# Two chunks per matmul in the triangular inverse of a chunked delta rule

## What is computed

```python
decay = jnp.exp(jnp.where(incl, gc[..., :, None] - gc[..., None, :], -jnp.inf))
kk = jnp.einsum('bhnid,bhnjd->bhnij', k, k)
a = jnp.where(strict, beta[..., :, None] * kk * decay, 0.0)
rhs = jnp.concatenate([beta[..., None] * v, (beta * jnp.exp(gc))[..., None] * k], axis=-1)
sol = lax.linalg.triangular_solve(eye + a, rhs, left_side=True, lower=True, unit_diagonal=True)
...
def step(state, xs):
    u_bar_c, w_c, qk_c, q_c, k_c, gl_c = xs
    u = u_bar_c - jnp.einsum('bhck,bhkv->bhcv', w_c, state)
    o = jnp.einsum('bhck,bhkv->bhcv', q_c, state) + jnp.einsum('bhcj,bhjv->bhcv', qk_c, u)
    state = gl_c[..., None, None] * state + jnp.einsum('bhck,bhcv->bhkv', k_c, u)
```

## Time and profile before

| | |
|---|---|
| median of three runs | 2509.23 us (2508.02 to 2509.98) |
| span of the profiled execution | 2508.8 us |
| PE busy | 2417.1 us, 96% of the span |
| DVE, ACT, POOL busy | 36%, 27%, 26% |
| one head of the delta loop | 94.4 us |
| one level of the inverse in it | 6.53 us |
| granted TensorE clock in the delta loop | full |

### The profile page before, as it was taken

One profiled execution on the slowest core, in us unless ns is written; L12 is line 12 of the kernel. 1 busy time (PEld: TensorE's weight loads), 2 busy tenths in 40 slices (PEclk: granted clock), 3 DMA queues, 4 the chain that ended last, 5 costly groups with the idle time before them and its releaser, 6 DMA issues.

```text
span 2508.8 us, 33006 instructions
## 1 busy us (share of the span) xinstructions
PE 2417.1 (96%) x12464; PEld 2031.8 (81%) x12464; DVE 905.7 (36%) x1069; ACT 688.6 (27%) x1204; POOL 660.2 (26%) x447
## 2 busy tenths in 40 slices
PE   5999999999799999999999999999899999999998
PEld 4787878787788888888888888887788888888887
DVE  4416262627554454454453112321422112211234
ACT  4333232324343543543452320011211001100112
POOL 6242232212111111111111323333233233323321
PEclk9999999999899999999999999999999999999999
DMA  5112121213010210220220443332111111111112
GB/s 119 37 42 85 51 84 50 75 42 109 18 59 17 59 59 12 63 59 10 66 67 26 160 137 119 119 101 70 39 49 43 50 50 42 50 51 45 48 44 82
DMA packets 219108, 157.30 MB, mean 63 GB/s; under 512 B 22744, under 2 KB 205208, under 8 KB 217520
## 3 DMA queue, kind: packets, MB, share of 16 engines
q1 hardware_dynamic: 206528, 106.05, 15.1%
q10 hardware_dynamic: 12528, 50.53, 5.6%
HBM read 137.49 MB, written 19.07 MB: 62 GB/s over the span
## 4 chain that ended last, share of the span: by engine, by line
PE 87%; DVE 5%; DVEq 2%; DMA 2%; issue 1%; ACT 1%; POOL 1%; SPq 0%; ACTq 0%; POOLq 0%
PE bank L198 62%; PE bank L988 5%; PE bank L1194 3%; PE bank L1204 3%; PE bank L1210 2%; DVEq L765 1%; DMA stat_b<-scr_stat 1%; PE bank L1151 1%; PE bank L602 1%; PE bank L1235 1%; DVE joint L769 1%; PE bank L1170 1%; PE bank L1222 1%; PE bank L1216 1%; PE bank L1176 1%
## 5 line engine op out<-in xcount | busy, mean ns | idle before, releaser
L198 PE MATMUL bank<-u_hi,w_hi 128*128 128x512 f32 x2176 | 907.3, 417 | 16.2 <-DVE u_lo L1642 7.2
L198 PE MATMUL bank<-u_hi,w_lo 128*128 128x512 f32 x2176 | 852.7, 392 | 0.0
L198 PE MATMUL bank<-u_lo,w_hi 128*128 128x512 f32 x2176 | 850.5, 391 | 0.0
L184 POOL CAST w_hi<-raw 128x1024 fp32r<-128x1024 f32 (+1 forms) x176 | 183.6, 1043 | 1768.6 <-PE bank L198 1522.7
L198 PEld LDWEIGHTS bank<-u_hi,w_hi 128*128 128x128 f32 x2176 | 411.7, 189 | 91.6 <-DVE u_lo L1642 8.8
L198 PEld LDWEIGHTS bank<-u_hi,w_lo 128*128 128x128 f32 x2176 | 409.5, 188 | 88.5
L198 PEld LDWEIGHTS bank<-u_lo,w_hi 128*128 128x128 f32 x2176 | 412.2, 189 | 69.4 <-issue 3.8
L186 POOL TENSOR_TENSOR w_lo<-raw,w_hi 128x1024 fp32r<-128x1024 f32 (+1 forms) x176 | 430.9, 2448 | 25.7 <-issue 0.7
L1756 DVE TENSOR_TENSOR tmp<-tmp,bank 128x512 f32<-128x512 f32 x44 | 30.2, 687 | 367.0 <-PE bank L198 367.0
L198 PE MATMUL bank<-v_hi,w_hi 128*128 128x512 f32 x352 | 137.3, 390 | 2.6 <-DVE tmp L1756 2.6
L198 PE MATMUL bank<-v_hi,w_lo 128*128 128x512 f32 x352 | 137.0, 389 | 0.0
(11 more groups left out here) (238 smaller groups left out, 2792.4 us busy)
## 6 DMA issues: line engine op xcount, KB each, us to landing
raw<-in_w_in SPq DMA_DIRECT2D x84, 512.0 KB, 3.8
stat_b<-scr_stat ACTq DMA_DIRECT2D x12, 1024.0 KB, 6.7
row<-scr_rows ACTq DMA_DIRECT2D x24, 512.0 KB, 4.9
raw<-in_w_gate SPq DMA_DIRECT2D x22, 512.0 KB, 3.8
raw<-in_w_up SPq DMA_DIRECT2D x22, 512.0 KB, 3.9
scr_gate<-tmp ACTq DMA_DIRECT2D x16, 512.0 KB, 2.9
tmp<-scr_gate ACTq DMA_DIRECT2D x16, 512.0 KB, 4.2
raw<-in_w_down SPq DMA_DIRECT2D x16, 512.0 KB, 3.7
```

The source lines that it names most:

```text
L184: nc.gpsimd.tensor_copy(hi[:, 0:kt, :], raw[slot][:, 0:kt, :])
L198: last = nc.tensor.matmul(bank[dst][:, :], wpart[slot][wp][:, k, :], rhs[ap][:, k, half * HALF:(half + 1) * HALF], start=k == 0 and (wp, a ...
```

## The change

Two neighbouring chunks share one matmul. Of `neg_a` only the right columns of the current level are taken, 64 of each chunk, and packed into `a_right` [128, 512]: a stationary tile of 128 columns then holds two chunks. The moving operand is the left columns of `inv` of both chunks (128 columns). The product has the wanted blocks of the two chunks on its diagonal; ACT copies only these into `half_pair`, a tile [128, 4, 128] whose other blocks are zeroed once. The transposes take only the right columns of `inv` (packed by DVE into `inv_right`), two chunks in one. The `d` matmul multiplies the paired transpose with `half_pair`, and the result lies in the bank as before, so that the masked copy is unchanged.

```diff
+        half_pair = dt_("half_pair", [P, NCH // 2, P])
+        a_right, inv_right = dt_("a_right", [P, HALF]), dt_("inv_right", [P, HALF])
...
         STEPS_AT = {4: ["ss"], 8: ["vt0"], 9: ["vt1"], 15: ["kt0"], 16: ["kt1", "kk0"], 17: ["kk1"], 18: ["qk0"],
-                    19: ["qk1"], 21: ["t00"], 22: ["t01"], 42: ["ub0", "ub1", "wt0", "wt1"], 61: ["os"], 63: ["on"]}
+                    19: ["qk1"], 20: ["t00"], 21: ["t01"], 41: ["tt0", "tt1"], 43: ["ub0", "ub1", "wt0", "wt1"],
+                    62: ["os"], 63: ["on"]}
         for level in range(1, 7):
-            for n_, x_ in enumerate("ydt"):
-                STEPS_AT[24 + 3 * (level - 1) + n_] = [f"{x_}{level}0", f"{x_}{level}1"]
+            STEPS_AT[22 + 3 * (level - 1)] = [f"y{level}"]
+            STEPS_AT[23 + 3 * (level - 1)] = [f"p{level}"]
+            STEPS_AT[24 + 3 * (level - 1)] = [f"d{level}0", f"d{level}1"]
         for c_ in range(NCH):
-            STEPS_AT[44 + 2 * c_] = [f"a{c_}"]
-            STEPS_AT[45 + 2 * c_] = [f"b{c_}"]
+            STEPS_AT[45 + 2 * c_] = [f"a{c_}"]
+            STEPS_AT[46 + 2 * c_] = [f"b{c_}"]
...
+            elif step[0] == "y":
...
+                pe.wait_ge(dl["ar"], h * 6 + level)
+                for q in range(NCH // 2):
+                    if level > 1 and q % 2 == 0:
+                        pe.wait_ge(dl["dtm"], n + (q // 2 - 1))
+                    last = mm(by_block(chunk(bank[Y0], q), level), chunk(a_right, q),
+                              side_columns(inv[:, 2 * q * P:2 * (q + 1) * P], level, 0), start=True, stop=True)
+            elif step[0] == "p":
+                level = int(step[1])
+                pe.wait_ge(dl["ir"], h * 6 + level)
+                for q in range(NCH // 2):
+                    last = tr(chunk(bank[X0], q), chunk(inv_right, q), ident[:, :])
+            elif step[0] == "d":
                 level, half = int(step[1]), int(step[2])
+                if half == 0:
+                    pe.wait_ge(dl["yc"], h * 6 + level)
+                    pe.wait_ge(dl["prc"], h * 6 + level)
+                for q in (2 * half, 2 * half + 1):
+                    last = mm(bank[Z0 + half][:, (q % 2) * P:(q % 2 + 1) * P], chunk(inv_t, q), half_pair[:, q, :],
+                              start=True, stop=True)
...
+            elif step[:2] == "tt":
+                half = int(step[2])
+                pe.wait_ge(dl["dtm"], h * 12 + (11 + half))
+                for c in range(4 * half, 4 * half + 4):
+                    last = tr(bank[X0 + half][:, (c % 4) * P:(c % 4 + 1) * P], chunk(inv, c), ident[:, :])
...
+            elif step[0] == "y":
+                level = int(step[1])
+                act.wait_ge(dl["y"], h * 6 + level)
+                y_now = bank[Y0][:, :].rearrange("p (q j) -> p q j", j=P)
+                f(half_pair[0:64, :, 0:64], y_now[0:64, :, 0:64], ACT.Copy)
+                f(half_pair[64:P, :, 64:P], y_now[64:P, :, 64:P], ACT.Copy).then_inc(dl["yc"], 1)
+                if level < 6:
+                    f(by_block(a_right[:, :], level + 1), side_columns(neg_a[:, :], level + 1, 1), ACT.Copy).then_inc(dl["ar"], 1)
+            elif step[0] == "p":
+                act.wait_ge(dl["pr"], h * 6 + int(step[1]))
+                f(inv_t[:, 0:HALF], bank[X0][:, :], ACT.Copy).then_inc(dl["prc"], 1)
...
+                if half == 1 and level < 6:
+                    dve.drain()
+                    v.tensor_copy(by_block(inv_right[:, :], level + 1),
+                                  side_columns(inv[:, :], level + 1, 1)).then_inc(dl["ir"], 1)
+            elif step == "t01":
+                dve.wait_ge(dl["t0c"], two + 2)
+                v.tensor_copy(by_block(inv_right[:, :], 1), side_columns(inv[:, :], 1, 1)).then_inc(dl["ir"], 1)
```

More of the change, by code:

```diff
@@ L1184, in delta_pe @@
                 last.then_inc(dl["t0"], 1)
-            elif step[0] in "ydt" and step[1] in "123456":
-                level, half = int(step[1]), int(step[2])
[L1187 to L1211, removed]
@@ new lines, in delta_pe @@
+            elif step[0] == "y":
+                level = int(step[1])
+                n = h * 12 + 2 * (level - 1)
+                if level == 1:
+                    pe.wait_ge(dl["t0c"], two + 2)
+                    pe.wait_ge(dl["a"], two + 2)
+                pe.wait_ge(dl["ar"], h * 6 + level)
[4 more added lines that the diff above has]
+                              side_columns(inv[:, 2 * q * P:2 * (q + 1) * P], level, 0), start=True, stop=True)
+                last.then_inc(dl["y"], 1)
+            elif step[0] == "p":
[3 more added lines that the diff above has]
+                    last = tr(chunk(bank[X0], q), chunk(inv_right, q), ident[:, :])
+                last.then_inc(dl["pr"], 1)
+            elif step[0] == "d":
+                level, half = int(step[1]), int(step[2])
+                if half == 0:
+                    pe.wait_ge(dl["yc"], h * 6 + level)
+                    pe.wait_ge(dl["prc"], h * 6 + level)
+                if level == 1:
+                    pe.wait_ge(dl["pt"], two + (half + 1))
+                for q in (2 * half, 2 * half + 1):
+                    last = mm(bank[Z0 + half][:, (q % 2) * P:(q % 2 + 1) * P], chunk(inv_t, q), half_pair[:, q, :],
+                              start=True, stop=True)
+                last.then_inc(dl["dt"], 1)
+            elif step[:2] == "tt":
[3 more added lines that the diff above has]
+                    last = tr(bank[X0 + half][:, (c % 4) * P:(c % 4 + 1) * P], chunk(inv, c), ident[:, :])
+                last.then_inc(dl["tt"], 1)
@@ L1212, in delta_pe @@
             elif step[:2] == "ub":
                 half = int(step[2])
-                pe.wait_ge(dl["ttc"], h * 12 + (11 + half))
+                pe.wait_ge(dl["ttc"], two + (half + 1))
                 for c in range(4 * half, 4 * half + 4):
@@ L1286, in delta_act @@
                 f(c4(inv, half), bank[X0 + half][:, :].rearrange("p (c t) -> p c t", t=P), ACT.Copy).then_inc(dl["t0c"], 1)
[L1287 to L1295, removed]
+                if half == 1:
+                    act.wait_ge(dl["a"], two + 2)
+                    f(by_block(a_right[:, :], 1), side_columns(neg_a[:, :], 1, 1), ACT.Copy).then_inc(dl["ar"], 1)
+            elif step[0] == "y":
+                level = int(step[1])
+                act.wait_ge(dl["y"], h * 6 + level)
[7 more added lines that the diff above has]
+                f(inv_t[:, 0:HALF], bank[X0][:, :], ACT.Copy).then_inc(dl["prc"], 1)
+            elif step[:2] == "tt":
+                half = int(step[2])
+                act.wait_ge(dl["tt"], two + (half + 1))
+                f(inv_t[:, half * HALF:(half + 1) * HALF], bank[X0 + half][:, :], ACT.Copy).then_inc(dl["ttc"], 1)
             elif step[:2] == "ub":
@@ L1443, in prepare_vec @@
                               ident[:, :].unsqueeze(1).broadcast_to([P, NCH, P]))
+                v.memset(half_pair[:, :, :], 0.0)
             dve.drain()
```

8 lines of the change are left out of this document (5 added, 3 removed).

## The result

The changed kernel takes **2452.24 us** (median, 2451.58 to 2453.41) against 2508.65 for the kernel before in the same runs: ratio 0.9772, 95% interval 0.9758 to 0.9786. It is 56 us faster; 73 were forecast, and the time lies inside the range of 2418 to 2462. It lies 2 us above the stretch that the forecast held most likely, 2425 to 2450.

A forecast was written before the change was run, and what follows sets the result against it. The inverse was taken as bound by PE issue: 8 x (12.26 saved - 3.04 new waits) = 73.8, less 0.5 for zeroing, is 73.3 us; span 2508.8 becomes 2435.5, median 2436 us, range 2418 to 2462.

The forecast's parts named there:

- What bounds the kernel: Delta loop's inverse: bound by what PE has to issue (busy 93.49 of 94.40 us per head), not its ACT/DVE chain.
- the price of the paired matmuls: y and d in each level: eight records cost 0.82 us instead of 1.70; four transposes cost 0.36 instead of 0.79.
- The rival by which the price follows the columns: y and d stay at 1.70 us with strided columns; each head 1.34 slower, 2520 us; chance 0.03.
- Net saving without waits: PE per head: 13.14 us saved in six levels, less 0.88 for the last full transpose: 12.26, or 98.1 in eight.
- The sum of the new waits: Four tighter hand-overs to PE: 1.35 + 0.79 + 0.60 + 0.30 = 3.04 us per head.
- first y: Head's first y waits for a_right, copied behind the last t0 copy: idle 0.68 us, with restart 0.79.
- first d: Level 1's d stands behind a dense copy on ACT as well: 0.60 us with the restart.
- second y: y's second half after the first d waits for merges; the first takes 0.73 instead of 0.44: 0.3 us with restart.
- item 1: d waits for ACT's copy of the packed transposes: 0.27 us in each of levels 2 to 6, 1.35 per head.
- the rival of slow packed copies: a_right's short runs cost ACT twice 0.63 us, delaying d, some 25 us in all: 2461, range 2450 to 2470; chance 0.15.
- POOL's block: Rival: POOL's subtraction blocks DVE's packed copy inv_right, p waits up to 1.5 us per head: 2448 us; chance 0.08.
- Border and places: Steps a and b move one j, b7 comes 0.69 us nearer the next head: no difference counted, within 1 us.

The follow-up runs named there:

- e4: Changed kernel with y matmuls given 64 moving columns instead of 128, every second chunk's result not computed: 2446.59 us in a single execution.
- e7: Changed kernel with ScalarE's copies reordered, packed transposes in two banks, inv_t copied in halves and d's first half waiting only for the first: 2416.40 us, ratio 0.9632.
- e2: Changed kernel with the two half_pair copies swapped, partitions 64 to 127 first: 2438.51 us, ratio 0.9716.
- e9: The e5 kernel with the first convolution's silu on ScalarE at j = 31 instead of 30: 2509.89 us, ratio 1.0000.
- e5: Kernel before with only the new places in the step table, matmuls and copies as they were: 2516.89 us, ratio 1.0024.
- e1: Changed kernel with each level's copy of the next a_right put behind the inv_t copy on ScalarE: 2435.83 us, ratio 0.9702.

## Why the prediction was right, and where it was off

- **What bounds the kernel, and the price of the paired matmuls: right.** 0.81 for y was 0.82 forecast, and e4 shows that the columns from 65 to 128 are free. The rival by which the price follows the columns is out, and with it 2520 us.
- **Net saving without waits, 12.26 us per head: right.** With groups of 0.81 and 0.35 it is 12.4; e7, with nearly all waits removed, has a head of 82.68, 11.7 below before.
- **The sum of the new waits, 3.04 us per head, was mis-sized; it is 5.0.** By the distances in the timeline above, with the slower groups behind a wait: first y 1.86 - 1.14 + 0.12 = 0.84 (forecast 0.79); first d 2.13 - 1.13 + 0.08 = 1.08 (0.60); second y 1.00 - 0.81 = 0.19 (0.30); d in levels 2 to 5 four times 1.70 - 1.13 + 0.08, together 2.60 (1.08); d in level 6, without an `a_right` copy, 0.32 (0.27). The term that failed is item 1: the estimate that four copies of different kinds overlap by 0.11 each, taken from a pair of equal copies in the earlier trace rows. The copies that start at partition 64 stop that (e2), so ACT takes the transposes 0.96 after them instead of 0.64. In level 3 the way on ACT from y's start to the copy of the transposes is 2.54 (926.71 to 929.25) against the forecast's 2.08: 0.39 of the difference are the three overlaps (the four copies start 0.39, 0.41 and 0.65 apart), 0.07 the first copy, which starts 1.09 after y (the row that the forecast cites gives 1.04, not 1.02). A second part is the hand-over from ACT to PE, 0.14 instead of the 0.06 that a VectorE row gave.
- **In numbers:** 1.74 us per head more than forecast, 13.9 in eight heads, of the 16 between 2436 and 2452. Of the rest, 0.8 lies between the spans (58.6 less instead of 73.3 less the 13.9), no more than the start of the heads varies. Some 1.6 is the way from span to median: the forecast took the median 0.4 above the span of the one profiled execution, and in the changed kernel it is 2.0 above (2452.24 to 2450.2). In that execution the time itself is 1.8 above the span (2451.97), as in every run that lists both; by that, the execution with the span of 2508.8 was slower than the median.
- **The range** holds the time in part by luck. 2452.24 lies outside the forecast's own 2425 to 2450 and inside the 2450 to 2470 of the rival of slow packed copies; the range reached so far because of that rival, and its cause did not come about.
- **The rival of slow packed copies** named the right queue for the wrong reason: `a_right` takes 0.63 us on ACT, as one of contiguous data; its short runs cost nothing that shows (0.63 was the price assumed; the first one of a head takes 0.67). It was the place in the queue and the missing overlap.
- **POOL's block:** the packed copy on DVE was never caught (0.43 us in all 48), as placed. The block of the tap stayed, 0.87 us of idle time as before; it moved from `state` to `u_now`, as forecast.
- **Border and places:** no new wait there in the changed kernel. That the places are free is shown by e9 for the kernel before; e5 shows that it holds only while nothing long stands on ACT ahead of a level's copies.

## What to carry to other kernels

A float32 matmul on 128 weight columns took as long with 128 moving columns as with 64: pack two such into one, and count records, not columns, up to that width (a record of 512 columns takes 0.23). When PE's groups shrink, the copies between them come onto the path: list for each engine the order of copies in one period, put the one that PE waits for first, and let the copies just before it start at the same partition as it does. A one-source operation of VectorE between SBUF tiles should not be placed beside a subtraction of GpSimd.

## What the runs showed of the hardware that was not expected

- ScalarE copies overlap the one before by about 0.1 us (0.60 long, 0.49 apart), but not behind a copy that starts at partition 64: 0.66 apart against 0.52, with the same instructions (e2). Where the first copy behind goes from a bank to SBUF, only that one is held (e1).
- From the end of ScalarE's `inv_t` copy to the matmul that waits for it pass 0.14 us (924.90 to 925.04), from VectorE's `state` 0.06. It is not a number of the engine: from ScalarE's first `a_right` copy to y it is 0.06 as well (915.99 to 916.05) in seven of the eight heads and 0.14 in the last. What sets it was not tested.
- A matmul of 64 columns takes as long as one of 128, 0.101 us per record (e4), with 128 weight columns in both.
